# Eight TensorE transposes of a group issued one by one between the matmuls of a tile, instead of in one row behind it

## What is computed

```python
u = rms_norm(h, g_mix); z = u @ w_in            # one projection feeds four mixers and the gates
o_nsa, o_s5, o_pool, o_ret = mixers(z)          # each 256 x 512
for j, o in enumerate((o_nsa, o_s5, o_pool, o_ret)):
    merged = merged + sigmoid(z_merge[j]) * (o @ w_branch[j])
h = h + merged @ w_out
v = rms_norm(h, g_mlp)
h = h + square(relu(v @ w_mlp_up)) @ w_mlp_down # 2048 -> 8192 -> 2048
h = h + sigmoid(h @ w_ple_gate) * (p @ w_ple_proj)
return rms_norm(h, g_final)
```

## Time and profile before

| | |
|---|---|
| median of 3 runs | 1638.1 us (1637.91 to 1638.48) |
| the profiled execution, its own time | 1638.13 us |
| span of that execution, first to last instruction | 1636.4 us |
| mean granted TensorE clock | 0.997 of 2.4 GHz |
| PE busy | 1615.0 us, 99% of the span |
| PEld busy | 1333.4 us, 81% |
| DVE busy | 1016.9 us, 62% |
| ACT busy | 766.6 us, 47% |
| matmuls of lines 362, 363, 364 | 2240 each |
| transposes of line 378 | 240 (30 groups of 8) |

### The profile page before, as it was taken

One profiled execution on the slowest core, in us unless ns is written; L12 is line 12 of the kernel. 1 busy time (PEld: TensorE's weight loads), 2 busy tenths in 40 slices (PEclk: granted clock), 3 DMA queues, 4 the chain that ended last, 5 costly groups with the idle time before them and its releaser, 6 DMA issues.

```text
span 1636.4 us, 20062 instructions
## 1 busy us (share of the span) xinstructions
PE 1615.0 (99%) x7614; PEld 1333.4 (81%) x7614; DVE 1016.9 (62%) x1220; ACT 766.6 (47%) x889; POOL 0.7 (0%) x5
## 2 busy tenths in 40 slices
PE   9999999999999999999999999999999999999996
PEld 7888878878888788888888888888888888888885
DVE  6547857646998997885555555555555555555564
ACT  7444446665344454444454434443344334444453
POOL 0000000000000000000000000000000000000000
PEclk9999999999999999999999999999999999999998
DMA  9687655655667668876666567655666666655653
GB/s 330 186 283 212 186 177 168 189 175 181 195 205 210 178 206 268 280 231 237 185 186 189 185 193 193 184 188 193 193 185 187 191 193 192 182 186 187 208 194 100
DMA packets 164433, 326.91 MB, mean 200 GB/s; under 512 B 10752, under 2 KB 16000, under 8 KB 163456
## 3 DMA queue, kind: packets, MB, share of 16 engines
q1 hardware_dynamic: 164352, 325.80, 64.2%
HBM read 315.27 MB, written 10.49 MB: 199 GB/s over the span
## 4 chain that ended last, share of the span: by engine, by line
PE 88%; DVE 9%; ACT 1%; issue 1%; DMA 1%; SPq 0%; ACTq 0%; DVEq 0%
PE ps L362 28%; PE ps L364 28%; PE ps L363 28%; DVE sb L345 3%; PE ps L378 2%; DVE sb L1488 1%; ACT sb L338 0%; PE ps L658 0%; PE ps L711 0%; PE ps L694 0%; DVE sb L1501 0%; DVE sb L1494 0%; DVE sb L1500 0%; DVE sb L1495 0%; DMA sb<-in_w_in 0%
## 5 line engine op out<-in xcount | busy, mean ns | idle before, releaser
L345 DVE TENSOR_TENSOR sb<-sb,sb 128x1024 fp32r<-128x1024 f32 x560 | 683.5, 1224 | 499.4 <-ACT sb L338 488.2
L338 ACT ACTIVATE sb<-sb 128x1024 fp32r<-128x1024 f32 x560 | 593.3, 1060 | 745.7 <-PE ps L364 725.3
L362 PE MATMUL ps<-sb,sb 128*128 128x512 f32 x2240 | 876.5, 391 | 0.5 <-DVE sb L345 0.5
L364 PE MATMUL ps<-sb,sb 128*128 128x512 f32 x2240 | 869.5, 388 | 0.0
L363 PE MATMUL ps<-sb,sb 128*128 128x512 f32 x2240 | 868.7, 388 | 0.0
L362 PEld LDWEIGHTS ps<-sb,sb 128*128 128x128 f32 x2240 | 420.6, 188 | 89.5 <-issue 4.9
L364 PEld LDWEIGHTS ps<-sb,sb 128*128 128x128 f32 x2240 | 420.4, 188 | 87.6
L363 PEld LDWEIGHTS ps<-sb,sb 128*128 128x128 f32 x2240 | 420.8, 188 | 84.0
L1613 DVE TENSOR_TENSOR sb<-sb 128x1024 f32<-128x1024 f32 x16 | 19.6, 1225 | 26.5 <-ACT sb L1094 26.5
L393 DVE TENSOR_TENSOR sb<-ps,sb 128x1024 fp32r<-128x1024 f32 x26 | 31.6, 1217 | 1.4 <-ACT sb L384 1.4
L1094 ACT ACTIVATE sb<-ps,sb 128x512 f32<-128x512 f32 x32 | 20.3, 685 | 24.7 <-PE ps L364 24.5
(11 more groups left out here) (225 smaller groups left out, 443.1 us busy)
## 6 DMA issues: line engine op xcount, KB each, us to landing
sb<-in_w_in SPq DMA_DIRECT2D x128, 512.0 KB, 3.8
sb<-in_w_up SPq DMA_DIRECT2D x128, 512.0 KB, 3.8
sb<-in_w_down SPq DMA_DIRECT2D x128, 512.0 KB, 3.7
sb<-in_w_mix SPq DMA_DIRECT2D x64, 512.0 KB, 4.5
sb<-in_w_branch SPq DMA_DIRECT2D x32, 512.0 KB, 5.4
sb<-in_w_out SPq DMA_DIRECT2D x32, 512.0 KB, 4.2
sb<-in_w_pg SPq DMA_DIRECT2D x32, 512.0 KB, 3.6
gate_mem<-sb SPq DMA_DIRECT2D x16, 512.0 KB, 5.1
```

What stands on the lines that cost most here:

```text
L338: act.activation(whi[:, j % RING, :], raw[:, j % RING, :], ACT.Copy).then_inc(hi_done, 1)
L345: eng.tensor_tensor(wlo[:, j % RING, :], raw[:, j % RING, :], whi[:, j % RING, :].bitcast(F32), ALU.subtract).then_inc(lo_done, 1)
L362: pe.matmul(o, xh, w_h, start=first and k == 0, stop=False)
L364: mm = pe.matmul(o, xl, w_h, start=False, stop=last and k == TK - 1)
```

## The change

`quad_in` is cut up: `quad_turn(i)` issues transpose number i of the eight, with the wait for `tp_lo` ahead of number 0 and the signal `tp_in` behind number 7. `products` takes a function `turn` and calls it behind the first and the second matmul of each three, eight times in a tile. The order of the 12 matmuls stays. `merged_in`, `hidden_in` and `last_in` now wait and then return that function; they are called ahead of `products` of the same tile (j == 1 or j == 3) behind which the row stood. The same is done for the MLP's groups. ACT, DVE and SP code isn't changed.

```diff
         def products(pe, u, j, g, par, x_hi, x_lo, kt, first, last, width=C, turn=None):
...
+                    n = 2 * (k * TT + tt)
                     pe.matmul(o, xh, w_h, start=first and k == 0, stop=False)
+                    if turn:
+                        turn(n)
                     pe.matmul(o, xh, w_l, start=False, stop=False)
+                    if turn:
+                        turn(n + 1)
                     mm = pe.matmul(o, xl, w_h, start=False, stop=last and k == TK - 1)
             mm.then_inc(tile_used, 1)
...
+        def quad_turn(pe, n, par, src, i):
+
+            if i == 0 and (not isinstance(n, int) or n >= 2):
                 pe.wait_ge(tp_lo, n - 1)
+            k, tt = i // TT, i % TT
+            mm = pe.transpose(aux[par][:, k * S + tt * P:k * S + (tt + 1) * P], src(k, tt), ident[:, :])
+            if i == 4 * TT - 1:
+                mm.then_inc(tp_in, 1)
...
             def merged_in(n):
                 pe.wait_ge(sg["merged_done"], n + 1)
-                quad_in(pe, TP_M + n, n % 2, lambda k, tt: merged[:, tt * C + k * P:tt * C + (k + 1) * P])
+                return lambda i: quad_turn(pe, TP_M + n, n % 2,
+                                           lambda k, tt: merged[:, tt * C + k * P:tt * C + (k + 1) * P], i)
...
-                    products(pe, U_BR + n, j, g, g % 2, o_hi, o_lo, j * TK, j % 2 == 0, j % 2 == 1)
-                    if j == 1 and n:
-                        merged_in(n - 1)
+                    products(pe, U_BR + n, j, g, g % 2, o_hi, o_lo, j * TK, j % 2 == 0, j % 2 == 1,
+                             turn=merged_in(n - 1) if j == 1 and n else None)
...
-                    products(pe, U_WO + n, j, g, g % 2, m_hi, m_lo, j * TK, j == 0, j == TPU - 1)
+                    turn = None
                     if n == 0 and j == 1:
-                        merged_in(NCH - 1)
+                        turn = merged_in(NCH - 1)
                     if j == 3 and n:
-                        hidden_in(n - 1)
+                        turn = hidden_in(n - 1)
+                    products(pe, U_WO + n, j, g, g % 2, m_hi, m_lo, j * TK, j == 0, j == TPU - 1, turn=turn)
```

More of the change, by code:

```diff
@@ L346, in split_lo, with products @@
                               ALU.subtract).then_inc(lo_done, 1)
-        def products(pe, u, j, g, par, x_hi, x_lo, kt, first, last, width=C):
+        def products(pe, u, j, g, par, x_hi, x_lo, kt, first, last, width=C, turn=None):
             if first:
@@ L372, in quad_in @@
         def quad_in(pe, n, par, src):
-            if not isinstance(n, int) or n >= 2:
+            for i in range(4 * TT):
+                quad_turn(pe, n, par, src, i)
+        def quad_turn(pe, n, par, src, i):
+            if i == 0 and (not isinstance(n, int) or n >= 2):
                 pe.wait_ge(tp_lo, n - 1)
[L376 to L379, removed]
+            k, tt = i // TT, i % TT
+            mm = pe.transpose(aux[par][:, k * S + tt * P:k * S + (tt + 1) * P], src(k, tt), ident[:, :])
+            if i == 4 * TT - 1:
+                mm.then_inc(tp_in, 1)
         def quad_hi(act, n, par, dst, scale=None):
@@ L555, in hidden_in @@
                 pe.wait_ge(grp_free, 2 * (G_WO + k + 1))
-                quad_in(pe, TP_H + k, (TP_H + k) % 2, lambda kk, tt: features(h, tt, 4 * k + kk))
+                return lambda i: quad_turn(pe, TP_H + k, (TP_H + k) % 2, lambda kk, tt: features(h, tt, 4 * k + kk), i)
             def last_in(k):
                 pe.wait_ge(grp_free, 2 * (G_PG - NCH + k + 1))
-                quad_in(pe, TP_P + k, (TP_P + k) % 2, lambda kk, tt: features(h, tt, 4 * k + kk))
+                return lambda i: quad_turn(pe, TP_P + k, (TP_P + k) % 2, lambda kk, tt: features(h, tt, 4 * k + kk), i)
             def gate_tile(t):
@@ L856, in mlp_group @@
                             pe.wait_ge(tp_lo, g * NCH + (TP_FF + (NCH if j else NCH - 1)))
-                        products(pe, g * (2 * NCH) + (U_FF + n), j, g * (2 * NCH) + (G_FF + n), (G_FF + n) % 2,
-                                 v_hi if up else f_hi, v_lo if up else f_lo, j * TK, j == 0, j == TPU - 1)
+                        turn = None
                         if first and n == 0 and j == 3:
-                            hidden_in(NCH - 1)
+                            turn = hidden_in(NCH - 1)
                         if j == 3 and 1 <= n <= NCH:
                             pe.wait_ge(sg["sq_done"], g * NCH + n)
-                            rl = relu[(n - 1) % 2]
-                            quad_in(pe, g * NCH + (TP_FF + n - 1), (TP_FF + n - 1) % 2,
-                                    lambda k, tt: rl[:, tt * C + k * P:tt * C + (k + 1) * P])
+                            turn = lambda i: quad_turn(
+                                pe, g * NCH + (TP_FF + n - 1), (TP_FF + n - 1) % 2,
+                                lambda k, tt: relu[(n - 1) % 2][:, tt * C + k * P:tt * C + (k + 1) * P], i)
                         if final and j == 3 and n > NCH:
-                            last_in(n - NCH - 1)
+                            turn = last_in(n - NCH - 1)
+                        products(pe, g * (2 * NCH) + (U_FF + n), j, g * (2 * NCH) + (G_FF + n), (G_FF + n) % 2,
+                                 v_hi if up else f_hi, v_lo if up else f_lo, j * TK, j == 0, j == TPU - 1, turn=turn)
             mlp_group(0, True, False)
@@ L878, in _ @@
                         pe.wait_ge(tp_lo, TP_P + (NCH if j else NCH - 1))
-                    products(pe, U_PG + n, j, g, g % 2, v_hi, v_lo, j * TK, j == 0, j == TPU - 1)
-                    if n == 0 and j == 3:
-                        last_in(NCH - 1)
+                    products(pe, U_PG + n, j, g, g % 2, v_hi, v_lo, j * TK, j == 0, j == TPU - 1,
+                             turn=last_in(NCH - 1) if n == 0 and j == 3 else None)
         @block.scalar
```

## The result

The changed kernel takes 1642.3 us (median of 9 runs, 1642.01 to 1642.89), the kernel before 1638.4 us (9 runs beside them, 1637.91 to 1638.94): ratio 1.0024, 95% interval 1.0016 to 1.0033. It is slower by 3.9 us. The time lies in the predicted range (1637.5 to 1645.0), but 2.3 us above the forecast of 1640.0, and just over the 0.2% up to which I called the forecast's case "the same".

A forecast was written before the change was run, and what follows sets the result against it. PE, busy 99% of the span, was taken to bound the kernel. The terms summed as 1638.13 + 0.3 (transposes) + 0 (aftermath) + 1.6 (four waits) = 1640.0 us, with a range of 1637.5 to 1645.0.

The forecast's parts named there:

- the forecast's case: Whole kernel: transposes no cheaper between matmuls, four waits exposed; 1640.0 us, bounds 1638.4 to 1641.3, chance 0.66.
- What bounds the kernel: Whole kernel: PE, busy 99% of the span, 88% of the chain; the 28 moved rows cost 25.8 us.
- The first rival: Mixed tiles: loads hide under the long matmuls, a transpose costs only its columns, 0.057 us; 1628 us, chance 0.09.
- a sign that it is wrong: A transpose between matmuls costing less than 0.1 or more than 0.12 us, or PE waiting anywhere else.
- The reason given for it: PE's transposes: the next 128x128 load, or something else not shrinking with moving columns, sets the 0.109 us each.
- The four waits: Branch stage and output projection's first unit: PE waits for `merged_done` ahead of the tile, 4 x 0.41 = +1.6 us.
- What comes later for others: `tile_used` comes 0.87 us later, ACT, DVE and SP work up to 0.9; `quad_lo` still 1.0 us early; cost 0.
- The transposes' own price: 28 moved groups: eight transposes between matmuls take 0.88 us against 0.87 in a row, +0.3 us in all.
- The aftermath: Some ten matmuls behind a row, each some 4 ns slow, 0.04 to 0.05 us; change 0, bounds -1.4 and +1.3 us.
- the second rival: Mixed groups: each of eight returns from transpose to matmul costs the whole 0.043 us; 1648.4 us; chance 0.17, partial included.
- Its partial form: Mixed groups: each return costs part of 0.043 us, deciding from 7 ns on; from 1641.4 us, within the rival's 0.17.
- The sum: Whole kernel: 1638.13 + 0.3 (transposes) + 0 (aftermath) + 1.6 (four waits) = 1640.0 us.

The follow-up runs named there:

- thin transposes: Transposes with 32 instead of 128 stationary columns: in a row on the kernel before, 1638.62 us; with 24 groups mixed and four in a row, 1639.57 us.
- e3: As the changed kernel, but merged_in groups in a row behind their tile, other transposes one by one behind the second and third matmul of each three; 1640.53 us.
- e4: As the changed kernel, but merged_in groups in a row behind their tile, other transposes in pairs behind the third matmul of each three; 1639.39 us.

## Why the prediction was right or wrong, point by point

- **What bounds the kernel, and that nothing is to be gained by hiding loads: right.** Between matmuls a transpose takes 0.11 to 0.14 us, never 0.057. The first rival (1628 us) is out. But the prediction named over 0.12 us for a transpose between matmuls as a sign that it is wrong, and half of them read 0.13 to 0.14; over the tile the mean is (3.70 - 12 x 0.227) / 8 = 0.122 us. The sign pointed at the two terms that were too small.
- **The reason given for it: half right.** I took the load for the pace, as I had looked only at a row with fewer moving columns. The thin transposes and the 256 columns of line 588 show that the 128 moving float32 columns set the same floor. The Trainium skill's load rule ("TensorE: Matmul & The Clock Gate", section "LDWEIGHTS (loading the stationary operand)"), 107 ns, agrees with one of the two floors. The 56 ns for 128 moving columns of its section "Back-to-back issue gap" doesn't hold for these float32 transposes, which took 109 ns even with a thin load.
- **The four waits: right.** 0.41 us late each, forecast 0.41; four places; none in the MLP, and the one-tile cover of the others held. 1.4 us net in the changed kernel, 1.7 alone; forecast 1.6.
- **What comes later for others: right.** The cut-up `quad_lo` of the first MLP unit ends at 835.04 + 1.66 = 836.70 us. Tile 6 loads at 837.47 and so streams at 837.70, 1.0 us later, as forecast, and no wait of PE for another engine is new but the four:

```profile
835.04 1.66 DVE L407 SCALAR_TENSOR_TENSOR sb<-ps,sb,sb 128x256 fp32r<-128x256 f32 x4 [0.23 <-ACT sb L397]
837.47 0.19 PEld L363 LDWEIGHTS ps<-sb,sb 128*128 128x128 f32 x1
```

- **The transposes' own price, +0.3 us: too small.** The full-size load between matmuls adds 0.04 us a group, 28 x 0.04 = 1.1 us. I had priced both neighbourhoods from the row's two ends, 0.23 and 0.11 us, read to 0.01 us. The new order has transpose, matmul, transpose in succession, which neither end shows: there 0.14 + 0.21 replace 0.11 + 0.23. An error of 10 ns a pair was within my reading, and rows to 0.01 us can't split it further; that it hangs on the load rests on the thin transposes.
- **The aftermath, its change taken as 0: this is the step that failed.** Its upper bound, +1.3 us, slow matmuls through the tile as well, was the right case: 0.05 us a group (what the thin transposes leave), 28 x 0.05 = 1.4 us (this size and the one of the load above hold to 0.01 us a group each, 0.3 us in all; their sum, 2.5 us, is measured directly). I chose "unchanged" though the reading I wrote down for the second rival, "a stretch of time behind a break", already meant that a break eleven matmuls earlier makes eleven more of them slow.
- **The second rival, a price for each break (1648.4 us): out.** The full 0.043 us for each of eight returns would have been 0.3 us a group, and 0.09 was measured. Its partial form, 12 ns for each return, fitted three kernels (the changed one, e3 and e4), and the two runs with two returns refuted it. As the prediction priced it, "in part" began at 1641.4 us, so the measured 1642.3 lies in this rival's span of times, for another reason than its own.
- **The sum.** 1638.1 + 1.4 (waits) + 1.1 (full loads in the mix) + 1.4 (aftermath) = 1642.0, measured 1642.3 (the profiled execution 1642.04). These terms were read from the runs afterwards, so the agreement of the sum is no test by itself; the tests are the run with the wait alone and the one with 24 mixed groups. The case was the likeliest one, with two of its terms 2.2 us too small together; that carried the time over the 0.2% line, to which I had given 0.17. The case's own upper end, 1641.3, was 1 us too low, the range held.

## What to carry to other kernels

Before moving a wait forward, ask what it now holds up: ahead of a tile it stops twelve matmuls that don't need the data, ahead of the first transpose only that. Putting short instructions between long ones can't gain while their moving columns alone fill the time that they take in a row; here the 128 columns were 0.11 us in either place. Whether a transpose with a cheaper stream would gain is open. Each interruption of this uniform stream made up to ten matmuls behind it a little slower, so one compact row was the cheapest form of those run. When a term has bounds on both sides, take the end that the mechanism you believe in implies, and read distances over hundreds of instructions where 10 ns decide.

## What the runs showed of the hardware that was not expected

- After both kinds of break seen here in the stream of 512-column fp32r matmuls, a row of transposes (2.31 us for ten) and a plain wait (2.08 us for nine), the matmuls take 0.231 instead of 0.227 us each on average. What causes it is open.
- Eight float32 transposes cost 0.87 us with 128 or with 32 stationary columns, and take 0.05 us each at 64x64, in a row. Eight float32 matmul instructions with 256 moving columns take 1.73 us.
- Changing between the full array and a 64x64 piece makes a transpose that lies between matmuls some 0.26 us dearer, for going and returning together.
